# The 1040 columns of a matmul block as pieces of 512, 512 and 16 instead of 352, 352 and 336

## The reference

```python
xn = rmsnorm(x, g_mix)
q, k, v, o, i, f, aq, ak, av, gate = split(xn @ w_in)
h_m = mlstm(q, k, v, i, f) normalised per head, times sigmoid(o)   # 4 heads
h_a = sliding_window_attention(rope(aq), rope(ak), av, sinks)       # 8 heads, window 128
ga, gb = split(sigmoid(gate))
x = x + (ga * (h_m @ w_a) + gb * (h_a @ w_b)) @ w_out
u = rmsnorm(x, g_ffn) @ w_up                                        # 1024 -> 2 * 2816
c = b_conv + sum over 3 taps of w_conv[tap] * shifted(u)
a, g = split(c)
x = x + (gelu(a) * g) @ w_down                                      # 2816 -> 1024
y = rmsnorm(x, g_final)
```

## Time and profile before

| | us |
|---|---|
| two timed executions | 3468.68 and 3469.83 |
| their median | 3469.26 |
| profiled execution, span from first to last instruction | 3472.4 |

### The profile page before, as it was taken

One profiled execution on the slowest core, in us unless ns is written; L12 is line 12 of the kernel. 1 busy time (PEld: TensorE's weight loads), 2 busy tenths in 40 slices (PEclk: granted clock), 3 DMA queues, 4 the chain that ended last, 5 costly groups with the idle time before them and its releaser, 6 DMA issues.

```text
span 3472.4 us, 46937 instructions
## 1 busy us (share of the span) xinstructions
PE 3205.9 (92%) x18027; PEld 2834.9 (82%) x18027; DVE 1484.5 (43%) x2139; ACT 854.0 (25%) x1346; POOL 422.8 (12%) x618
## 2 busy tenths in 40 slices
PE   8999999999859999799999999699997999999995
PEld 4555555555549999699999999599996999999995
DVE  3454544545323123454453535542234544535345
ACT  1222222222222222221221212332222212212122
POOL 1212212122100001110110101200011101101012
PEclk9999999999759999899999999899998999999998
DMA  5101011010132112111111111231121111111112
GB/s 191 39 20 38 25 32 38 19 38 25 40 120 50 46 45 86 37 49 43 43 48 50 46 46 40 107 111 48 43 85 37 54 44 37 48 50 46 49 37 77
DMA packets 129750, 184.65 MB, mean 53 GB/s; under 512 B 43170, under 2 KB 84130, under 8 KB 129570
## 3 DMA queue, kind: packets, MB, share of 16 engines
q1 hardware_dynamic: 123362, 183.51, 17.0%
q10 hardware_dynamic: 6336, 0.45, 0.1%
HBM read 155.42 MB, written 29.52 MB: 53 GB/s over the span
## 4 chain that ended last, share of the span: by engine, by line
PE 62%; DVE 4%; issue 2%; ACT 1%; SPq 1%; DMA 1%; POOL 0%; DVEq 0%; POOLq 0%; ACTq 0%
PE f_ps L1244 62%; DVE f_cg L1399 1%; DVE f_xres L1395 1%; DVE f_wl L1390 1%; DVE f_xl L1471 0%; ACT f_wh L1288 0%; PE f_st L1253 0%; POOL f_ca L1553 0%; DMA o_conv<-f_xres 0%; SPq L1167 0%; SPq L1168 0%; DVE f_cg L1481 0%; DVE f_cg L1479 0%; DVE f_ca L1503 0%; DMA f_raw<-in_w_gate 0%
## 5 line engine op out<-in xcount | busy, mean ns | idle before, releaser
L1390 DVE TENSOR_TENSOR f_wl<-f_raw,f_wh 128x1024 fp32r<-128x1024 f32 x234 | 278.0, 1188 | 1345.2 <-ACT f_wh L1288 1345.1
L1244 PE MATMUL f_ps<-f_xh,f_wh 128*128 128x352 f32 (+1 forms) x3264 | 701.1, 323 | 97.9 <-DVE f_xl L1418 57.4
L1244 PE MATMUL f_ps<-f_xh,f_wl 128*128 128x352 f32 (+1 forms) x3264 | 698.4, 322 | 0.0
L1244 PE MATMUL f_ps<-f_xl,f_wh 128*128 128x352 f32 (+1 forms) x3264 | 697.4, 322 | 0.0
L1244 PEld LDWEIGHTS f_ps<-f_xh,f_wh 128*128 128x128 f32 x3264 | 553.7, 190 | 101.4 <-issue 92.5
L318 PE MATMUL pp<-wmix,xn 128*128 128x512 f32 (+1 forms) x1360 | 569.6, 574 | 0.0
L1244 PEld LDWEIGHTS f_ps<-f_xl,f_wh 128*128 128x128 f32 x3264 | 551.8, 190 | 0.0
L1244 PEld LDWEIGHTS f_ps<-f_xh,f_wl 128*128 128x128 f32 x3264 | 549.9, 189 | 0.0
L1288 ACT ACTIVATE f_wh<-f_raw 128x1024 fp32r<-128x1024 f32 x234 | 234.6, 1002 | 1199.5 <-PE f_ps L1244 1112.3
L318 PEld LDWEIGHTS pp<-wmix,xn 128*128 128x128 f32 x1360 | 265.1, 199 | 262.8 <-issue 255.0
L1244 PE MATMUL f_ps<-f_gh,f_wh 128*128 128x352 f32 (+1 forms) x1056 | 229.7, 326 | 25.4 <-DVE f_gl L1514 25.4
(11 more groups left out here) (223 smaller groups left out, 3263.7 us busy)
## 6 DMA issues: line engine op xcount, KB each, us to landing
f_raw<-in_w_up SPq DMA_DIRECT2D x88, 512.0 KB, 3.7
f_raw<-in_w_dn SPq DMA_DIRECT2D x48, 384.0 KB, 3.0
f_raw<-in_w_gate SPq DMA_DIRECT2D x34, 512.0 KB, 3.6
xt<-in_x SPq DMA_DIRECT2D x19, 512.0 KB, 4.9
xn_rows<-xn SPq DMA_DIRECT2D x18, 512.0 KB, 3.5
o_y<-f_xres SPq DMA_DIRECT2D x16, 520.0 KB, 3.1
wmix<-in_w_mix SPq DMA_DIRECT2D x4, 2048.0 KB, 15.7
mixer_rows<-ht SPq DMA_DIRECT2D x16, 512.0 KB, 3.8
```

The source lines that it names most:

```text
L1244: mm = pe.matmul(ps[s][:, i, 0:cn], w[s][:, k * P:k * P + P], x[:, k0 + k, c0:c0 + cn], start=(k == 0 and n == 0), stop=(k == K - 1 and n ...
L1390: dve.tensor_tensor(wl[s][:, 0:width], raw[s][:, 0:width], wh[s][:, 0:width].bitcast(F32), ALU.subtract).then_inc(ev("w_lo"), 1)
```

## The change

The pieces are 512, 512 and 16 columns. The first two then are exactly the prompt's columns and the third the samples', so `evacuate` loses its middle copy, and the gate tile's slices follow. `two` takes its width from `PIECES` and needs no edit: its parts are 1024 and 16 columns.

```diff
-PIECES = [(0, 352), (352, 352), (704, T - 704)]
+PIECES = [(0, 512), (512, 512), (1024, T - 1024)]
...
                 act.activation(u[:, 2:2 + 2 * n].rearrange("p (a b) -> p a b", a=2), p[:, 0:2, 0:n], ACT.Copy)
-                act.activation(u[:, 2 + 2 * n:2 + PT], p[:, 2, 0:PT - 2 * n], ACT.Copy)
                 act.activation(samp(u)[:, :, 2:2 + STEPS],
                                p[:, 2, PT - 2 * n:T - 2 * n].rearrange("p (s j) -> p s j", s=BS), ACT.Copy
                                ).then_inc(ev(f"ps_read{s}"), 1)
...
-                    g = sga[:, 0:704].rearrange("p (a b) -> p a b", a=2) if len(p.shape) == 3 else sga[:, 704:T]
+                    g = sga[:, 0:1024].rearrange("p (a b) -> p a b", a=2) if len(p.shape) == 3 else sga[:, 1024:T]
```

## The result

The changed kernel takes 3919.85 us (two runs, 3919.77 to 3919.92) against 3469.26: a ratio of 1.129 with a 95% interval of 1.127 to 1.131, slower. The forecast was 3921. The profiled execution has a span of 3917.8 us, 445.4 more than before.

A forecast was written before the change was run, and what follows sets the result against it. TensorE's issue rate was taken as the bound: 447.2 us of triple growth, +5.6 for the lower clock and -1.4 for the copies make +451.4 us, 3923.8 on the span and 3921 us timed. The range was 3770 to 4045 us.

The forecast's parts named there:

- TensorE's issue rate is the bound, and triples are the unit: Second half, line 1244: a triple is three matmuls under one weight tile, 474.6 ns; 4704 triples take 2232 us.
- A 512-column matmul at 230.4 ns: Large pieces of a triple: 230.4 ns each, the middle of 227.1 by the instruction and 233.6 by the column.
- The small piece at 112 ns: 16-column matmul: from its start to effective work of the next takes 112 ns, with the weight load exposed.
- 150 triples hidden: Waits for the last hidden tile hide 108 triples' growth, the second norm's steps 42; 4554 grow by 98.2 ns, +447.2 us.
- Lower clock, +5.6 us: Slow spells after each long wait: an estimated 55 triples grow by 200 ns and not 98, +5.6 us.
- The copies, -1.4 us: Evacuations: 172 ns less each, on the path only where the down product waits, 8 times, -1.4 us.
- The sum: Whole kernel: 447.2 + 5.6 - 1.4 = +451.4 us, giving 3923.8 us on the profiled span and 3920.7 as timed median.
- rival (b): Small piece, its weight load hidden: triple 459 ns, 3398 us, or 3384 us by the skill's gap rule; chance 0.04.
- (a): Matmul after the small piece starts on part of its weights: small piece 57 ns, 3667 us; chance 0.06.
- (c): Triple's extra 13.8 ns goes by the instruction, load hidden: 474.7 ns, no change, 3469 us; chance 0.04.
- (d): Gaps in TensorE's stream open the clock gate, clock low for a tenth of triples: +232 us, 4153 us; chance 0.04.

The follow-up runs named there:

- the timed pair: The changed kernel with its 1024-element copy made as two of 512, timed beside the changed kernel on one chip: 3918.18 against 3919.76 us.

## Why the prediction was right, point by point

- **TensorE's issue rate is the bound, and triples are the unit.** Right. 4704 triples x (573.4 - 474.6) = +464.8 us before what waits take back.
- **A 512-column matmul at 230.4 ns.** Measured 0.23 us in the timeline and 232.4 ns by the run with the small piece for one pair only. Of the two readings I averaged, the one by the column holds (0.454 x 512 = 232.5) and the one by the instruction (227.1) doesn't. My middle was 2 ns short of it.
- **The small piece at 112 ns.** Measured 109, by the triple and by the two of three that were taken out. It was read from loads of another line behind matmuls of 8, 16 and 65 columns, and it carried over. The two errors, 4 ns too little for the large pieces and 3 too much for the small one, nearly cancel: 572.8 forecast, 573.4 measured. That part of the closeness is luck.
- **150 triples hidden.** The wait for the last hidden tile gave back 11.0 us, of which 108 x 0.0988 = 10.7 is growth; the norm's steps gave back 3.5 us against 4.1 forecast. Missed: the column sums' wait for GpSimd went from 32.4 us (the line below, from the waits of the kernel before) to 29.3, which is 3.1 us more given back.

```profile
PE f_st L1253 <- POOL f_ca L1553: 32.4, 4, 9.4
```

- **Lower clock, +5.6 us.** Wrong in its net. The price of a slow triple is right: from 2397.78 to 2402.78 us, at a granted clock of 0.50, 14 matmuls take 5 us, 1071 ns per triple, against 1067 forecast and 867 before. But the number of slow triples was taken to stay, and it fell. By the granted clock in windows of 1 us, line 1244 is busy at the lower level for about 50 us before and 44 us after; I estimate from this 57 triples before and 41 after. Over full clock they cost 57 x 0.392 = 22.3 us before and 41 x 0.498 = 20.4 after, a net of -1.9 and not +5.6 us. The last section shows spells that are gone.
- **The copies, -1.4 us.** Wrong, though small. The failed step, as put: "That is on the path only where the down product waits". It isn't on the path even there, since VectorE's subtraction for the next weights ends later than the evacuation. The size was off as well: the copies overlap, so the evacuation became only 0.07 us shorter (2.11 to 2.04 us) and not 0.172. The value of the term is 0 within what can be measured, shown by the starts in all three kernels and by the timed pair.
- **The sum.** 464.8 - 11.0 - 3.5 - 3.1 - 1.9 (estimated) = 445.3 us, against 445.4 in the spans; forecast 451.4. So the forecast of the growth was 6 us too large, 1.3% of it. That the time itself came out at 3919.85 against 3920.7 is luck: I took the timed median to lie 3.1 us below the profiled span, as before the change, and after it the profiled execution was timed at 3919.92, 2.1 above its span of 3917.8. The two executions behind 3469.26 were low ones; on the chips of the later runs the kernel before took 3473 to 3474 us, and the changed one 446 more (3919.76 against 3473.65).
- **The two rules.** A matmul of 16 columns costs 109 ns here, where the Trainium skill ("TensorE: Matmul & The Clock Gate", "Back-to-back issue gap") has a floor of about 25 ns for small ones; the measurement decides. The Trainium skill's section "LDWEIGHTS (loading the stationary operand)" of that page gives the columns over 1.2 GHz, 107 ns for 128, and with it the runs agree (106 to 114): the two have to be read together. The section "Back-to-back issue gap" of the Trainium skill's page says so itself, which rival (b) passed over: in a stream of weight loads and matmuls both set the spacing, and its formula has no budget for the load.
- **The rivals.** (a), a price of 57 ns, would have been 3667; the early recorded start is real in the changed kernel too (0.03 us), but the longer duration behind it gives the time back. (b) and (c) needed a hidden load; the floor is about the same with 16, 128 and 224 columns. (d), a clock that falls in the stream: in the free stretch the granted clock is 1.00.

## What to carry to other kernels

Where every matmul brings its own weight load, choose pieces by the shortest one: in this kernel none may be shorter than the load's 110 ns, some 240 columns at 2.4 GHz in float32r (224 did not hide it, 272 did). Three pieces near 350 columns cost what their columns cost, and filling banks with 512, 512 and a rest of 16 costs 100 ns for each rest. Read the rate from counts in a stretch without idle time, since a busy share of 100% hides a wait for weights in the matmul's own duration.

## What the runs showed that I had not expected

**The excess over 2.4 GHz goes by the column.** With all loads hidden, a triple of 1040 columns takes 471.5 to 479.0 ns, against 433.3 at one column per cycle. Each of these triples has three matmuls, so they can't tell a price per column from one per instruction. The 232.4 ns of a matmul of 512 columns can: 0.454 ns per column, as in the fastest of these triples, where a price per instruction would give 227.1. At 1.2 GHz the excess is absent. That it shifts with the split (the table above) may point to reads of the moving operand; no run shows this.

**Behind the shorter waits the clock stayed up.** The down product's first matmuls after the wait for the last hidden tile (in brackets the idle time): the first and the third group of a block in the kernel before, then the first and the last in the changed one, each with the window of 5 us behind it.

```profile
1601.82 0.74 PE L1244 MATMUL f_ps<-f_gh,f_wh 128*128 128x352 f32 x3 [2.45 <-DVE f_gl L1514]
1601.82:1606.82 5.00, 5.00 (x22) 5.00 (x23) 1.75 (x2) 1.06 (x1) 0.00 (x0) 0.66 0.00 0
...
2020.94 0.74 PE L1244 MATMUL f_ps<-f_gh,f_wh 128*128 128x352 f32 x3 [2.50 <-DVE f_gl L1514]
2020.94:2025.94 5.00, 5.00 (x31) 5.00 (x32) 2.01 (x3) 1.06 (x1) 0.00 (x0) 1.00 0.00 0
```

```profile
1704.14 0.74 PE L1244 MATMUL f_ps<-f_gh,f_wh 128*128 128x512 f32 x3 [0.96 <-DVE f_gl L1513]
1704.14:1709.14 5.00, 5.00 (x26) 4.23 (x27) 1.79 (x2) 1.06 (x1) 0.00 (x0) 1.00 0.00 0
...
2397.78:2402.78 5.00, 5.00 (x14) 4.13 (x15) 0.42 (x1) 1.06 (x1) 0.00 (x0) 0.50 0.00 0
```

All eight places, in both blocks:

| | idle before | granted clock in the next 5 us |
|---|---|---|
| before, first three groups | 2.45 to 2.50 us, 6 times | 0.66 or 0.67 four times, 1.00 twice |
| before, last group | 5.30 us, twice | 0.66 and 0.63 |
| after, first three groups | 0.92 to 0.96 us, 6 times | 1.00 each time |
| after, last group | 4.38 us, twice | 0.50 each time |

The other runs fill in the sizes between: of six waits of 2.47 to 2.51 us (pieces of 320, 320 and 400) five were followed by a fall, of six of 2.05 to 2.11 us (the small piece for one pair only) two were followed by a fall, of six of 1.69 us (third piece of 128) two, of 18 of 0.92 to 0.99 us (the changed kernel again, three copies, the small piece between) none. The shorter the wait, the rarer the fall, but the idle time alone doesn't decide: in the kernel before, after the same 2.5 us, the clock fell in the first two groups of each block and stayed up in the third.

Over the 12 us behind each of the eight waits, the mean granted clock gives about 20 us at the lower level before and 12 after, although the two long waits are followed by longer spells than before. Over the whole half the time at the lower level with line 1244 at work fell by only 6 us; the spells elsewhere differ too, and for those no cause is shown.
